# Modulations of a two-part network: one multiply-and-sum per 128 of them, in place of columns on VectorE and sums on TensorE

## The reference

```python
# shapes: c [1, 1024], ada_w [2, 1024, 9216], ada_b [2, 9216], final_ada_w [1024, 2048]
m = silu(c) @ ada_w[l] + ada_b[l]          # 9 * 1024 modulations a layer: shift, scale, gate for 3 parts
...
u = rmsnorm(x, gain) * (1 + scale) + shift
x = x + factor * (1 + gate) * part(u)      # factor 0.5 or 1
...
shift, scale = split(silu(c) @ final_ada_w + final_ada_b)
```

## Time and profile before

| what | value |
|---|---|
| median of 3 runs | 2096.02 us |
| the profiled execution's own time | 2095.03 us |
| its span, first to last instruction | 2093.7 us |
| mean granted clock of TensorE | 0.968 |
| TensorE busy | 1966.9 us (94%) |
| VectorE busy | 1415.6 us (68%) |
| ScalarE busy | 944.0 us (45%) |
| read from DRAM | 385.93 MB, 185 GB/s over the span |

### The profile page before, as it was taken

How to read it: one execution, slowest core, us unless ns; L and a number is a source line. 1 busy time by engine, 2 the same in 40 slices (tenths; PEclk the granted TensorE clock), 3 DMA queues, 4 the chain that set the end, 5 groups by cost and what they waited for, 6 DMA issues and landing times.

```text
span 2093.7 us, 35020 instructions
## 1 busy us (share of the span) xinstructions
PE 1966.9 (94%) x15328; PEld 1885.4 (90%) x15328; DVE 1415.6 (68%) x2250; ACT 944.0 (45%) x1268; POOL 39.9 (2%) x48
## 2 busy tenths in 40 slices
PE   8999898899899986999999899999999999999998
PEld 8988788899788885999999789999999999889998
DVE  6677677776776785766776866667766775765444
ACT  5554454455545543433445334334433445434333
POOL 0000100000000000000000000000000000000000
PEclk9998999999999998999999999999999999999999
DMA  8554457575463664577556345676577656344551
GB/s 279 178 179 149 141 179 229 154 241 161 144 205 111 222 205 163 196 239 240 192 188 216 111 165 178 239 240 234 182 241 242 202 176 206 105 130 146 184 182 61
DMA packets 342394, 389.24 MB, mean 186 GB/s; under 512 B 8417, under 2 KB 325985, under 8 KB 342113
## 3 DMA queue, kind: packets, MB, share of 16 engines
q1 hardware_dynamic: 342240, 387.00, 56.5%
HBM read 385.93 MB, written 1.05 MB: 185 GB/s over the span
## 4 chain that ended last, share of the span: by engine, by line
PE 68%; DVE 20%; ACT 9%; DMA 2%; issue 1%; SPq 0%; POOL 0%; DVEq 0%; ACTq 0%
PE bank L700 21%; PE bank L701 20%; PE bank L702 20%; DVE weights_split L875 6%; ACT weights_split L869 4%; DVE mod_sum L856 2%; PE bank L764 2%; ACT map L1311 1%; DVE xbc L2177 1%; DVE map_stat L1499 1%; PE bank L829 1%; ACT map L1317 1%; DMA weights<-in_w_in 1%; PE bank L925 1%; DVE map L1493 1%
## 5 line engine op out<-in xcount | busy, mean ns | idle before, releaser
L875 DVE TENSOR_TENSOR weights_split<-weights,weights_split 128x2048 fp32r<-128x2048 f32 (+2 forms) x306 | 653.0, 2134 | 363.3 <-ACT weights_split L869 362.8
L869 ACT CAST weights_split<-weights 128x2048 fp32r<-128x2048 f32 (+2 forms) x306 | 542.7, 1774 | 168.1 <-PE bank L702 121.1
L700 PE MATMUL bank<-u,weights_split 128*128 128x256 f32 x2048 | 595.1, 291 | 18.7 <-DVE u L2195 10.1
L701 PE MATMUL bank<-u,weights_split 128*128 128x256 f32 x2048 | 584.3, 285 | 0.0
L702 PE MATMUL bank<-u,weights_split 128*128 128x256 f32 x2048 | 584.0, 285 | 0.0
L700 PEld LDWEIGHTS bank<-u,weights_split 128*128 128x128 f32 x2048 | 393.0, 192 | 25.6 <-DVE u L2195 13.3
L701 PEld LDWEIGHTS bank<-u,weights_split 128*128 128x128 f32 x2048 | 394.7, 193 | 0.5 <-issue 0.5
L702 PEld LDWEIGHTS bank<-u,weights_split 128*128 128x128 f32 x2048 | 393.9, 192 | 0.0
L700 PE MATMUL bank<-y,weights_split 128*128 128x256 f32 (+1 forms) x1168 | 339.6, 291 | 7.7 <-ACT b_k L895 4.2
L701 PE MATMUL bank<-y,weights_split 128*128 128x256 f32 (+1 forms) x1168 | 333.0, 285 | 0.0
L702 PE MATMUL bank<-y,weights_split 128*128 128x256 f32 (+1 forms) x1168 | 332.9, 285 | 0.0
(11 more groups left out here) (288 smaller groups left out, 2021.1 us busy)
## 6 DMA issues: line engine op xcount, KB each, us to landing
weights<-in_w_in SPq DMA_DIRECT2D x76, 1024.0 KB, 7.8
weights<-in_ada_w SPq DMA_DIRECT2D x72, 1024.0 KB, 5.1
weights<-in_ffn_wg SPq DMA_DIRECT2D x44, 1024.0 KB, 5.8
weights<-in_ffn_wu SPq DMA_DIRECT2D x44, 1024.0 KB, 7.7
weights<-in_ffn_wd SPq DMA_DIRECT2D x44, 1024.0 KB, 8.5
weights<-in_w_merge SPq DMA_DIRECT2D x24, 1024.0 KB, 7.8
weights<-in_w_out SPq DMA_DIRECT2D x20, 1024.0 KB, 5.4
weights<-in_w_ple_gate SPq DMA_DIRECT2D x8, 1024.0 KB, 7.7
```

The costliest lines, as they stand in the source:

```text
L700: pe.matmul(out, left[0], right[0], start=start, stop=False, **more)
L701: pe.matmul(out, left[0], right[1], start=False, stop=False, **more)
L869: act.do.copy(split[:, 0, 0:n], raw[:, 0:n]).then_inc(*self.act_wrote.inc(("weights", key)))
L875: dve.do.tensor_tensor(split[:, 1, 0:n], raw[:, 0:n], split[:, 0, 0:n].bitcast(F32), ALU.subtract).then_inc(*self.dve_wrote.inc(("weights" ...
```

## The change

`ada_w` is laid out on the host with each modulation's 1024 weights in one row: a slot holds two times 128 modulations, one a partition, 8 KB a partition. `cond` becomes silu(c) as 128x1024, the same in every partition. VectorE makes 128 modulations by one instruction: it multiplies the weights with `cond`, in place, and sums along the row, starting from the bias. TensorE's sums, `mod_sum` and its bank's use are gone, and with them the two steps after the last group. `c` and the lambda vectors are loaded as tensors of their own, ahead of the constants; both layers' lambdas are computed at the start. The mixers' accumulator ring uses the bank under another name.

```diff
@@ Order.modulations
             self.add("modulate", n, 1)
             self.mod_open = False
-            self.mods_known = 2 * n
+            self.mods_known = 2 * n + 2
             yield
             yield
-        self.add("modulate", len(ADA), 0)
-        yield
-        self.add("modulate", len(ADA), 1)
-        self.mods_known = 2 * len(ADA)
-        yield
@@ Order.first_layer
             self.add("constants")
             self.mods_pause = False
-        self.add("lambda", l)
+            for layer in range(DEPTH):
+                self.add("lambda", layer)
@@ tiles
-        self.mod_sum = self.new_ring([self.tile(f"mod_sum{i}", [P, 256]) for i in range(2)])
-        self.cond = self.tile("cond", [P, DC])
+        self.cond = self.tile("cond", [P, D])
@@ tensor_modulate: the whole function, and its two calls
-        for i in range(2):
-            last = pe.do.matmul(bank[:, i:i + 1], total[:, i * P:(i + 1) * P], self.k("ones", 0), start=True, stop=True)
...
@@ vector_modulate
-            dve.wait_ge(self.filled, ("modulations", n - 1))
-            dve.do.tensor_tensor(self.mods[:, 2 * n - 2:2 * n], self.mod_banks.tile(n - 1)[:, 0:2], bias,
-                                 ALU.add).then_inc(*self.dve_wrote.inc(("modulations", n - 1)))
...
-            dve.do.tensor_scalar(total[:, :], view[:, 0, :], self.cond[:, 0:1], None, ALU.mult).then_inc(
-                *self.dve_wrote.inc())
-        total = self.mod_sum.tile(n)
-        for k in (range(DC // 2, DC) if half else range(1, DC // 2)):
-            dve.wait_ge(self.dve_wrote, LAST)
-            dve.do.scalar_tensor_tensor(total[:, :], view[:, k, :], self.cond[:, k:k + 1], total[:, :], ALU.mult,
-                                        ALU.add).then_inc(*self.dve_wrote.inc(*[("mod_sum", n)] * (k == DC - 1)))
+        dve, col = self.dve, 2 * n + half
+        l, j = ADA[n]
+        bias = self.s(f"ada_b{l}", 1, 2 * j + half) if l < DEPTH else self.s("final_ada_b", 1, 2 * j + half)
+        rows = self.raw.tile(("ada", n))[:, half * D:(half + 1) * D]
+        dve.wait_ge(self.loaded[self.raw.place.get(("ada", n), 0)], ("ada", n))
+        dve.wait_ge(self.act_wrote, "cond")
+        dve.do.tensor_tensor_reduce(rows, rows, self.cond[:, :], 1.0, bias, ALU.mult, ALU.add,
+                                    self.mods[:, col:col + 1]).then_inc(
+            *self.dve_wrote.inc(*[("modulations", n)] * half))
         if half:
-            self.raw.emptied(("ada", n), self.dve_wrote, ("mod_sum", n))
+            self.raw.emptied(("ada", n), self.dve_wrote, ("modulations", n))
@@ scalar_first, "constants"
-                act.do.activation(self.cond[:, :], self.s("c", 8), ACT.Silu).then_inc(*self.act_wrote.inc("cond"))
+                act.do.activation(self.cond[:, :], self.cond[:, :], ACT.Silu).then_inc(*self.act_wrote.inc("cond"))
@@ sync_load
-            source = (self.a["ada_w"][l] if l < DEPTH else self.a["final_ada_w"])[:, j * 256:(j + 1) * 256]
...
+            sp.do.dma_start(slot[:, :], self.a["ada"][at]).then_inc(*loaded.inc((what, at)))
@@ sync_first, "constants"
                 sp.do.dma_start(self.small[:, :], self.a["small"]).then_inc(*self.parameters_loaded.inc())
+                sp.do.dma_start(self.cond[:, :], self.a["c"]).then_inc(*self.parameters_loaded.inc())
+                sp.do.dma_start(self.b["lam_rows"], self.a["lambda"]).then_inc(*self.parameters_loaded.inc())
@@ on the host
+def modulation_rows(a):
+
+    rows = [np.asarray(w).T for w in a["ada_w_2"]] + [np.asarray(a["final_ada_w_2"]).T]
+    rows = np.concatenate(rows, 0).reshape(len(ADA), 2, P, D)
+    return np.ascontiguousarray(rows.transpose(0, 2, 1, 3)).reshape(len(ADA), P, 2 * D)
...
+    arrays["ada"] = modulation_rows(given)
+    arrays["c"] = np.ascontiguousarray(np.broadcast_to(given["c_2"].reshape(1, D), (P, D)))
+    arrays["lambda"] = np.ascontiguousarray(np.broadcast_to(given["diff_lambda"].reshape(1, -1), (P, 512)))
```

More of the change, by code:

```diff
@@ L91 @@
              ("conv_b", 8), ("ret_gn", 4), ("ssm_norm", 4), ("d_skip", 4), ("dt_bias", 8),
-             ("a_log", 8), ("lambda", 256)]
+             ("a_log", 8)]
 SMALL_SIZES = [(f"{n}{l}", s) for l in range(DEPTH) for n, s in PER_LAYER]
-SMALL_SIZES += [("c", 8), ("final_ada_b", 16), ("final_norm", 8)]
+SMALL_SIZES += [("final_ada_b", 16), ("final_norm", 8)]
 SMALL_AT, SMALL_N = columns(SMALL_SIZES)
@@ L954, in first_tiles @@
         self.diagonal = sb("diagonal", [P, P])[:, :]
-        b["lam"] = sb("lam", [P, 8])
-        b["lam_prod"] = b["tmp"][:, 0:2 * DIFF_QK].rearrange("p (a d) -> p a d", a=2)
+        b["lam"] = sb("lam", [P, DEPTH, 8])
+        b["lam_prod"] = b["tmp"][:, 0:4 * DIFF_QK].rearrange("p (l a d) -> p l a d", l=DEPTH, a=2)
+        b["lam_rows"] = self.gate.tiles[1][:, :]
         width = columns(CONST_SIZES["first"])[1]
@@ L974, in tensor_first @@
                 self.tensor_norm(*at)
-            elif what == "modulate":
-                self.tensor_modulate(*at)
             elif what == "constants":
@@ L1415, in vector_lambda @@
     def vector_lambda(self, l):
-        dve, lam, prod = self.dve, self.b["lam"], self.b["lam_prod"]
+        dve, lam, prod = self.dve, self.b["lam"][:, l, :], self.b["lam_prod"][:, l, :, :]
         lam_init = 0.8 - 0.6 * math.exp(-0.3 * l)
-        lf = self.s(f"lambda{l}", 256).rearrange("p (a b d) -> p a b d", a=2, b=2)
-        dve.do.tensor_tensor(prod[:, :, :], lf[:, :, 0, :], lf[:, :, 1, :], ALU.mult).then_inc(*self.dve_wrote.inc())
+        lf = self.b["lam_rows"][:, 256 * l:256 * (l + 1)].rearrange("p (a b d) -> p a b d", a=2, b=2)
+        dve.do.tensor_tensor(prod, lf[:, :, 0, :], lf[:, :, 1, :], ALU.mult).then_inc(*self.dve_wrote.inc())
         dve.wait_ge(self.dve_wrote, LAST)
-        dve.do.tensor_reduce(lam[:, 0:2], prod[:, :, :], AX.X, ALU.add).then_inc(
+        dve.do.tensor_reduce(lam[:, 0:2], prod, AX.X, ALU.add).then_inc(
             *self.dve_wrote.inc(("lambda_sums", l)))
@@ L1526, in vector_branch_c @@
             dve.wait_ge(self.dve_wrote, LAST)
-            dve.do.scalar_tensor_tensor(z, both, b["lam"][:, 5:6], z, ALU.mult, ALU.mult).then_inc(
+            dve.do.scalar_tensor_tensor(z, both, b["lam"][:, l, 5:6], z, ALU.mult, ALU.mult).then_inc(
                 *self.dve_wrote.inc(("weighed", "c", l, g)))
@@ L1588, in sync_load @@
         sp, slot = self.sp, self.raw.take((what, at))
+        sp.wait_ge(*self.raw.free((what, at)))
+        loaded = self.loaded[self.raw.place[what, at]]
         if what == "weights":
             source, rows, cols = self.panels[at]
-        else:
-            (l, j), rows, cols = ADA[at], D, 256
-            source = (self.a["ada_w"][l] if l < DEPTH else self.a["final_ada_w"])[:, j * 256:(j + 1) * 256]
-        kc = rows // P
-        sp.wait_ge(*self.raw.free((what, at)))
-        sp.do.dma_start(slot[:, 0:kc * cols].rearrange("p (k n) -> p k n", k=kc),
-                        source.rearrange("(k p) n -> p k n", p=P)).then_inc(
-            *self.loaded[self.raw.place[what, at]].inc((what, at)))
+            kc = rows // P
+            sp.do.dma_start(slot[:, 0:kc * cols].rearrange("p (k n) -> p k n", k=kc),
+                            source.rearrange("(k p) n -> p k n", p=P)).then_inc(*loaded.inc((what, at)))
+        else:
+            sp.do.dma_start(slot[:, :], self.a["ada"][at]).then_inc(*loaded.inc((what, at)))
     def sync_first(self):
```

35 lines of the change are left out of this document (7 added, 28 removed).

## The result

The changed kernel takes 2032.24 us, the median of 4 runs (2022.23 to 2039.97), against 2095.36 us for the kernel before (4 runs, 2093.64 to 2101.29). The ratio is 0.9688, 95% interval 0.9671 to 0.9705. The profiled execution took 2039.97 us, with a span of 2038.7 us.

A forecast was written before the change was run, and what follows sets the result against it. The prediction took TensorE to bound the feed-forwards and VectorE and ScalarE in turn the attention and mixer stretches. Its sum was 2095.0 - 25.5 - 17 + 2 = 2054.5, given as 2055 us, range 2033 to 2076.

The forecast's parts named there:

- TensorE's sums, 25.5 us: Modulations' one-column sums on TensorE: removing them gains 0.44 us at each of 58 places on the chain, 25.5 us.
- VectorE, 17 us: Half modulations at 27 chain places shorten to 1.26 us each, 21 us; four fifths kept, 17 us gained.
- the loads: Loads of `ada_w`, in 8 KB rows instead of eight of 1 KB: nothing counted, 2 us of gain kept for the range.
- the start, +2: First 20 us, DMA-bound: 0.52 MB more to load and a longer silu of c cost 2 us, between 1 and 5.
- the check of the sum: Check on the 27 half modulations' chain time: L856 comes to 49.5 us, against the page's 2.4% of the span, 50 us.
- Half rate: Rival on VectorE's multiply-and-sum: two cycles an element, about 2.3 us from start to start; 2084 us in all, chance 0.08.
- The rule of half throughput: Skill's rule for VectorE's multiply-and-sum: two SBUF sources wider than bf16 run at half throughput; the case for half rate.
- the third panel: Sign at the start: the third weight panel's landing moves from 14.97 to about 16.8 us.
- ScalarE next: Rival: ScalarE's copies take VectorE's place on the chain, only 4 us of VectorE's gain stays; 2067 us, chance 0.14.
- The clock: Rival in the attention streams, 70 to 135 us and alike: TensorE falls to 1.2 GHz, +68 us, 2122 us, chance 0.03.
- The low end of the range: Whole kernel: far bounds of all terms give 2036 us, less 3 us for TensorE keeping 2.4 GHz: 2033 us.

The follow-up runs named there:

- e1: The kernel before without TensorE's sums over the partitions, the bias added to a column of `mod_sum` instead: 2069.01 us, ratio 0.9874.
- e2: The changed kernel with two one-column TensorE sums put back for each modulation but the last, result unused: 2065.52 us, ratio 0.9853.
- h1: The kernel before with 64 bytes of padding behind `cond`, giving distance 192 between streamed tiles and split weights: 2064.17 us, ratio 0.9862.
- e4: The changed kernel with 64 bytes of padding behind `cond`, so all streamed tiles lie where they lay before (distance 128): 2051.55 us, ratio 0.9782.
- g1: The changed kernel with c, lambda and the first modulation moved behind the second a_v panel, plus 64 bytes of padding behind `cond`: 2052.51 us, ratio 0.9781.
- g3: The changed kernel with each multiply-and-sum over 128 of its 1024 elements, plus 64 bytes of padding behind `cond`: 2040.91 us, ratio 0.9728.
- f3: The changed kernel with 64 bytes of padding ahead of the split weights: streamed tiles where they lay before, distance 64 kept: 2037.99 us, ratio 0.9695.
- e3: The changed kernel with c, the lambda rows and the first modulation moved behind the second a_v panel: 2040.7 us, ratio 0.9741.
- e6: The changed kernel with the rows of `ada_w` loaded in 8 pieces of 1 KB a partition: 2039.99 us, ratio 0.9716.
- e5: The kernel before with 192 bytes of padding behind `cond`, giving distance 64: 2082.39 us, ratio 0.9936.
- g2: The changed kernel with `ada_w` loaded in pieces of 1 KB, plus 64 bytes of padding behind `cond`: 2053.61 us, ratio 0.9786.

## Why the prediction was right and wrong

**TensorE's sums, 25.5 us: right.** e1 gives 26.4 us for them alone, e2 27.9 us when they are put back, and 0.44 to 0.45 us per modulation came out on two bases, 0.48 at h1's fastest spacing. Reading a cycle with and without the step was better than reading the busy time.

**VectorE, 17 us, the loads and the start, +2: right as a sum.** e4 less e1 is (0.9874 - 0.9782) x 2095.4 = 19 us, where 15 were forecast. The half modulation takes 1.20 us (1.26 forecast). (The 2.4% of L856 in the check of the sum is the chain's own figure; the earlier trace rows rounds it to 2%.) Half rate, which would have been 2.3 us, is excluded by the rows at 64.22 and 65.42. The rule of half throughput of the Trainium skill's "Vector Engine (DVE) Microarchitecture Reference" ("Points that are easy to get wrong") names the scalar-tensor-tensor form with two SBUF sources that are not bf16. This instruction, which the trace calls CUSTOM_DVE_ANT_0, also has two such sources and a sum, and does not run at half rate at 128x1024. The start was late as forecast at the third panel (16.60 for about 16.8), by 5.0 us at the panel after the first modulation, and by 3.6 us at 58 us. e4 is 2.2 us behind e1 there (60.69 against 58.45), close to the 2 of the sum. That the kernel after is level with before by 170 us is in large part VectorE's gain: the chain of before passes through five half modulations up to there, three with 0.6 us saved and two with 0.95, 3.7 us in all. What the start costs by the end stays open: g1 is no faster than e4, but its interval is wider than 2 us, and it moves the modulations too. The loads' larger rows are worth nothing that shows, as counted.

**ScalarE next: right in kind.** Its share of the chain rises from 9% to 10%, the wait of the split (all forms) for it from 362.8 to 433.6 us, and in g3 a further saving of VectorE shows for some 12 halves only.

**The clock: no fall where the rival had put it**, 1.00 over 70 to 135 us. In other places it differs, and the prediction had no term for that. Over 16 to 28 us it is 0.86 in the kernel after and 1.00 in before and in e4, whose next panel comes 1.5 us sooner (29.25 against 30.75). Over 220 to 232 us it is the kernel before that falls, to 0.72, behind a landing that is no longer on the chain after the change, and by their size this wait (2 to 3 us) and this fall (7 us at half clock, so some 3 us) are most of the 6 us of lead won there. The mean clock of the four executions is 0.971 in e4 and 0.968 in e1, some 13 us less at half clock. That is up to 7 of the 19 us above, an estimate that takes TensorE as the limit in all of them. How much of it counts was not isolated.

**What failed** is a step that the prediction did not have. Its sum holds everything not named at the durations of before, the matmuls' spacing above all, and it read the cycle of the last feed-forward, 17.09 us, as what TensorE takes "without a modulation". It is what TensorE takes at that distance between its operands. The tiles' changed sizes stood in the diff, with their consequence of 64 bytes, and I took the layout for neutral. With the addresses of before the change comes to 2051.55 us (2050 by its ratio), 3.5 to 5 us from the forecast; the missing 14 to 20 us are the move. The low end of the range, 2033, had no term for a matmul that starts sooner after the one before it: 16.96 us a cycle where the sum had 17.09.

**The best version** is f4, the change with 128 bytes of padding: 2007.82 us, 0.9607 (0.9549 to 0.9664), below both kernels. Its own runs reach from 1999.63 to 2025.45.

## What to carry to other kernels

When a change resizes a tile, work out how far every tile behind it moves, and measure the change once with padding that puts them back: only then is the time the change's own. Where TensorE runs without gaps, try a few paddings between streamed tiles and stationary ones; here one line was worth 29 us on the old kernel and 37 on the new one at the old addresses by the ratios (31 and 44 by the medians). And take a whole cycle with and without the step as the price of a small instruction on a full engine.

## What was unexpected in the hardware

With the granted clock at 1.00 and no gap on TensorE, the 128x256 matmuls of three-pass fp32r products start 120.0, 118.7, 117.8 or 113.3 ns apart (cycles of 17.28, 17.09, 16.96 and 16.32 us by 144), and which of these it is goes with the remainder by 256 bytes of the distance between the streamed tile and the weights: 0 and 96 give the first, 128 the second, 64 the third or the fourth, and 192 the fourth in f4's profiled execution, whose others are up to 26 us slower. That it is the distance and not the address of the streamed tile is shown at 64 alone (f3). The remainder by 128 does not order them: 0 and 128 differ by 14 us, 64 and 192 by 30 by the medians (16 and 23 by the ratios).

At 64 and 192 one execution differs from the next in time, and at 64 a feed-forward from the next within one execution (e3's profile has 16.32 twice, then 16.96 twice; e6's has 16.32 once, then 16.96), while in the kernels without sums a feed-forward keeps its spacing to its end. In h1, whose sums come once a cycle, it changes with every cycle; in e2 and e5, with sums at distance 64, it does not. That the sums flip it, and that the cause lies in how reads of the two operands meet in the memory, is only a guess; no run looked at it. What picks the spacing at these distances stays open, and so does the 17.28 us of e4's last feed-forward at a distance where the others (e1, g1, g2, g3) have 17.09 throughout.
